# Latent attention: the weights' scaling by the reciprocal of their sums on GpSimd instead of VectorE

## The reference

```python
def mla_attention(q, k, v):
    # q, k: (B, S, 8, 96); v: (B, S, 8, 64)
    for blk in range(S // 128):
        qs, qe = blk * 128, (blk + 1) * 128
        logits = jnp.einsum('bqhd,bkhd->bhqk', q[:, qs:qe], k[:, :qe]) * scale
        logits = jnp.where(k_chunk <= q_chunk, logits, -jnp.inf)
        probs = jax.nn.softmax(logits, axis=-1)
        outs.append(jnp.einsum('bhqk,bkhd->bqhd', probs, v[:, :qe]))
```

## Time and profile before

| | us |
|---|---|
| median of three runs | 2461.8 |
| the profiled execution, first to last instruction (its span) | 2460.0 |
| TensorE busy in the span | 2419.9 (98%) |
| VectorE busy | 1705.1 (69%) |
| ScalarE busy | 1050.4 (43%) |
| GpSimd busy | 139.0 (6%) |
| the attention of the units, from its first scaling to its last values product | about 340 to 487 |

### The profile page before, as it was taken

One profiled execution on the slowest core, in us unless ns is written; L12 is line 12 of the kernel. 1 busy time (PEld: TensorE's weight loads), 2 busy tenths in 40 slices (PEclk: granted clock), 3 DMA queues, 4 the chain that ended last, 5 costly groups with the idle time before them and its releaser, 6 DMA issues.

```text
span 2460.0 us, 29760 instructions
## 1 busy us (share of the span) xinstructions
PE 2419.9 (98%) x11494; PEld 1921.0 (78%) x11494; DVE 1705.1 (69%) x2072; ACT 1050.4 (43%) x1495; POOL 139.0 (6%) x227
## 2 busy tenths in 40 slices
PE   8999999999999999999999999999999999999997
PEld 6887755588888888888788777788878888888885
DVE  5237888846877778698873665455588877786888
ACT  5225676624433333333542333343356333334336
POOL 1001100000000010000001000000001000100001
PEclk9999999999999999999999999999999999999999
DMA  5110000132433381600134122233444533715103
GB/s 220 52 43 22 2 1 1 52 137 107 150 119 121 103 307 53 222 1 18 52 100 151 43 78 70 72 133 134 148 150 175 171 103 103 263 45 194 47 1 137
DMA packets 76245, 252.22 MB, mean 103 GB/s; under 512 B 6320, under 2 KB 6368, under 8 KB 76080
## 3 DMA queue, kind: packets, MB, share of 16 engines
q1 hardware_dynamic: 43792, 131.08, 16.7%
q0 software_dynamic: 32320, 119.32, 13.0%
HBM read 186.78 MB, written 62.91 MB: 102 GB/s over the span
## 4 chain that ended last, share of the span: by engine, by line
PE 75%; DVE 10%; issue 4%; ACT 2%; DVEq 0%; ACTq 0%
PE ps L2717 23%; PE ps L3126 20%; PE ps L3164 18%; PE ps L3294 6%; DVE opQ_lo L2132 1%; DVE opQ_lo L2129 1%; DVE spot L2174 1%; DVE ql_raw L2169 1%; DVE Pb L1999 1%; PE ps L3221 1%; PE ps L3240 1%; PE ps L2965 1%; PE ps L3230 1%; PE ps L2839 0%; PE ps L2902 0%
## 5 line engine op out<-in xcount | busy, mean ns | idle before, releaser
L3164 PE MATMUL ps<-opQ_hi 128*128 128x512 f32 x896 | 350.3, 391 | 2.8 <-DVE opQ_lo L2132 2.8
L3164 PE MATMUL ps<-opQ_hi,opQ_lo 128*128 128x512 f32 x896 | 348.7, 389 | 0.0
L3164 PE MATMUL ps<-opQ_lo,opQ_hi 128*128 128x512 f32 x896 | 348.7, 389 | 0.0
L2717 PE MATMUL ps<-opP_hi,w_hi 128*128 128x512 f32 x638 | 199.2, 393 | 2.4 <-DVE w_lo L1620 0.7
L3164 PEld LDWEIGHTS ps<-opQ_hi 128*128 128x128 f32 x896 | 168.2, 188 | 42.1 <-DVE opQ_lo L2132 7.1
L2717 PE MATMUL ps<-opP_lo,w_hi 128*128 128x512 f32 x638 | 196.6, 389 | 0.0
L2717 PE MATMUL ps<-opP_hi,w_lo 128*128 128x512 f32 x638 | 196.4, 389 | 0.0
L3164 PEld LDWEIGHTS ps<-opQ_hi,opQ_lo 128*128 128x128 f32 x896 | 168.2, 188 | 35.1
L3164 PEld LDWEIGHTS ps<-opQ_lo,opQ_hi 128*128 128x128 f32 x896 | 168.2, 188 | 34.7 <-issue 0.2
L1276 ACT ACTIVATE opQ_hi<-spot 128x1024 fp32r<-128x1024 f32 x80 | 84.9, 1062 | 235.9 <-PE ps L3164 196.8
L884 ACT ACTIVATE w_hi<-w_stage 128x1024 fp32r<-128x1024 f32 x104 | 109.4, 1051 | 174.4 <-PE ps L2717 145.4
(11 more groups left out here) (441 smaller groups left out, 4763.0 us busy)
## 6 DMA issues: line engine op xcount, KB each, us to landing
w_stage<-in_w_stream SPq DMA_DIRECT2D x104, 512.0 KB, 3.7
h_spill<-T POOLq DMA_DIRECT2D x56, 512.0 KB, 4.5
pair_raw<-in_w_stream SPq DMA_DIRECT2D x26, 1024.0 KB, 5.8
spot<-in_w_stream SPq DMA_DIRECT2D x24, 1024.0 KB, 7.0
spot<-h_spill POOLq DMA_DIRECT2D x24, 1024.0 KB, 9.5
qh_raw<-in_w_stream SPq DMA_DIRECT2D x8, 1024.0 KB, 11.6
ql_raw<-h_spill POOLq DMA_DIRECT2D x8, 1024.0 KB, 7.5
g_spill<-T POOLq DMA_DIRECT2D x16, 512.0 KB, 2.9
```

The source lines that it names most:

```text
L2717: mm = pe.matmul(ps[:, psum + half, :], weight, operand[:, k, half * HALF:(half + 1) * HALF], start=(begin and x == 0 and weight is wh and ...
L3164: mm = pe.matmul(ps[:, down_bank(sc, f) + m, :], weight, operand, start=(g == 0 and kt == 0 and weight is wh and operand is hi), stop=(g = ...
```

## The change

The scaling leaves `normalise`, which keeps the reciprocal and its waits. GpSimd gets a loop over the 64 units, behind its additions: it waits for the reciprocal of the unit and scales the weights in place. The semaphores keep their meaning; `mha["pn"]` is now raised by GpSimd.

```diff
@@ GpSimd @@
                 ins.then_inc(g["pexp"], 1)
+
+            for u, (pr, qt, par) in enumerate(QBLOCKS):
+                width = (qt + 1) * P
+                pool.wait_ge(mha["rs"], u + 1)
+                pool.tensor_scalar(Pb[:, u % 4, 0:width], Pb[:, u % 4, 0:width], rsum[:, u % 4:u % 4 + 1], None, ALU.mult)\
+                    .then_inc(mha["pn"], 1)
@@ VectorE @@
             def normalise(u):
 
-                pr, qt, par = QBLOCKS[u]
-                width = (qt + 1) * P
                 v.wait_ge(mha["exp"], u + 1)
                 if u >= 4:
                     v.wait_ge(mha["pn"], u - 3)
                 v.reciprocal(rsum[:, u % 4:u % 4 + 1], esum[:, u % 4:u % 4 + 1]).then_inc(mha["rs"], 1)
-                v.wait_ge(mha["rs"], u + 1)
-                v.tensor_scalar(Pb[:, u % 4, 0:width], Pb[:, u % 4, 0:width], rsum[:, u % 4:u % 4 + 1], None, ALU.mult)\
-                 .then_inc(mha["pn"], 1)
```

## The result

| | before | after |
|---|---|---|
| median of the runs | 2461.8 us | 2489.8 us |
| the profiled execution's span | 2460.0 us | 2488.2 us |

The ratio is 1.0114, with a 95% interval of 1.0102 to 1.0126: slower by 28 us. The forecast was 2464 with a range of 2459 to 2476, so it was wrong, and by more than the slow rival (2477) allowed.

What follows compares the result with a forecast made beforehand. TensorE was taken as nearly full in attention, VectorE next. Four groups' shifts, −1.0 + 0.9 − 0.4 + 1.7, plus 1.2 of latency gave +2.4 us: 2460.0 to 2462.4, and 1.8 for the median, 2464.2; range 2459 to 2476.

Steps and rivals of the forecast that it cites:

- slow rival: GpSimd's scaling runs at the two-input rate, 2.03 ns an element: about +15 us, 2477; chance 0.30 with a half-slow case.
- Added: the GpSimd instruction: Price of one scaling on GpSimd, estimated near the memset's: 0.15 us + 0.86 ns an element, 1.03 us at 1024.
- upper bound: Highest price kept for a GpSimd scaling, from two-input rows at some 2.03 ns an element: 2.08 us at 1024.
- the prediction's own line between +2.4 and +15: Loss against GpSimd's time per element, from the forecast's +2.4 us to +15 at 2.03 ns; 1.45 ns gives some +8.7.
- No change: The outcome that the time stays within about 0.2%, 4.9 us, of the kernel before; chance 0.61.
- Added: a lock: In attention, 13 two-input VectorE extras starting just ahead of GpSimd's scaling hold it back 1.22 to 1.28 us each.
- Added: a hand-over: GpSimd starts 0.08 us after the VectorE instruction it awaits, against 0.04 within VectorE; uncovered latency costs 1.2 us in all.
- Removed from VectorE: 64 scalings, 33 us, leave VectorE in the attention stage; at most TensorE's 6.1 us of waiting could return.
- The cover: TensorE's other work hides the scaling in steps with a values product and the next; three places a group lose 0.3 us.
- The point of decision: The forecast is wrong if TensorE's wait for the scaling, 6.1 us before, falls under 2 us or rises over 12.

Runs made afterwards that it cites:

- e1: The changed kernel with GpSimd scaling only the first quarter of each unit's weights, the rest left unscaled: 2463.1 us beside 2461.6 for the kernel before.
- e3: The changed kernel with GpSimd's scaling written as a product of two tensors, the reciprocal broadcast along the row: 2472.1 us.
- e13: The changed kernel with one line moved, so VectorE takes the reciprocal of unit u+1 ahead of the row maximum of u+2: 2473.9 us.
- e8: The kernel before with seven chosen units scaled on GpSimd as a two-input product, the rest on VectorE: 2462.3 us beside 2460.0.
- e10: The kernel before with only the 16 units u % 4 = 2 scaled on GpSimd, each scaling also waiting for the one before it: 2474.8 us.
- e12: The kernel before with units u % 4 = 2 scaled on GpSimd, counted on its own semaphore, without waiting for the previous scaling: 2475.0 us.
- e9: The kernel before with only the 16 units u % 4 = 0 scaled on GpSimd, each scaling also waiting for the one before it: 2469.6 us.
- e11: The kernel before with units u % 4 = 0 scaled on GpSimd, counted on its own semaphore, without waiting for the previous scaling: 2467.4 us.
- e2: The changed kernel with GpSimd scaling only the first half of each unit's weights, the rest left unscaled: 2468.5 us.
- e15: The kernel before, scaling on VectorE, with reciprocal and scaling of unit u+1 moved ahead of the maximum of u+2: 2468.7 us.
- e14: The changed kernel with GpSimd scaling by a product of two tensors and the reciprocal moved ahead of the next maximum: 2463.8 us beside 2460.7.

## Why the prediction was wrong

**The step that failed** is "Added: the GpSimd instruction": "I take 0.15 us + 0.86 ns an element, an estimate: 1.03 us at 1024". It measured 0.28 us + 2.5 ns, 2.84 at 1024, above the upper bound of 2.08 too, and with it TensorE waited 30.5 us for scalings in place of 6.1. The memset was no near row: it writes only, with no arithmetic. e1 shows that the forecast held for a scaling of about the duration assumed. The rule that was weighed there, that of GPSIMD Engine Reference of the Trainium skill (Elementwise — side-by-side cycle accounting) with an estimated 0.88 us for 1024, is contradicted by the same rows, 2.84 us. Beside the slow rival the prediction set GPSIMD Engine Reference of the Trainium skill (When to use GPSIMD), which sends elementwise work to VectorE; the direction agrees with the trace. But that section calls work with one input roughly line-rate, and here it took 3.8 times VectorE's 0.753 us at 1024.

**The slow rival** had the right sign and a chance of 0.30. On the prediction's own line between +2.4 and +15, 1.66 ns an element gives an estimated 11 us, and e3 measured 10.3. Its rate was too low for the kernel after, but that is not all: on the same line 2.5 ns gives an estimated 20 us, and 28 were measured. The other 8 are the cover, below, and the lower clock. "No change" had 0.61 of the chances because both ends of the bound came from operations of another kind.

**Added: a lock.** It held where it was applied. The scalings behind two-input extras are longer by some 0.9 us (3.16 for 2.20, 3.42 for 2.52), the extras keep 1.27 and 1.20 us, and the one-input long reciprocals lock nothing, which the prediction assumed and SBUF — State Buffer of the Trainium skill (Who interferes with whom) says; the 0.93 us at 411.07 agree. Its net share of the time is small, 2.6 us by the medians, and not told from nothing. "Each time the later one stood until the earlier had finished" is too wide: e13's extra behind a one-input scaling did not stand.

**Added: a hand-over.** 0.10 us against the predicted 0.08.

**Removed from VectorE.** Busy time as predicted, 89.43. That it would return only what stood behind the scaling, 6.1 us at most, agrees with e8: 2.6 us of wait came back, and GpSimd's own delays took 4.0.

**The cover** ("in steps with V, and the step after, V covers it. That leaves three places in each group") failed as well, though at the assumed duration it didn't matter (e1). TensorE waited in 32 places, where it had waited in 15 before and 12 were to grow, and e10 and e12 show the "covered" units to cost more than the bare ones of e9 and e11. The cover was counted from the values product's length, without asking when in it the reciprocal comes.

**The point of decision.** "TensorE's wait ... over 12" was a good mark: of the kernels with scalings on GpSimd, those whose medians are over 0.2% longer are those from e2's 12.5 us up. e15 shows its limit, since there the delay stands before the scores.

What stays open: e14's median is 3.0 us longer with only 0.3 us more wait for scalings. Its profiled execution took 2462.2 us, among the shortest of runs that go up to 2468.2, and its span of 2460.5 is 0.5 over that of the kernel before; what the longer ones do, no trace shows. Open, too, is the exact share of the lock, since taking the extras out also takes out work, and how the 8 us beyond the prediction's line divide between the cover and the clock.

## What to carry to other kernels

A free engine is worth nothing to a chain that it makes slower: before moving an instruction off a busy engine, find the ring that it stands in and compare the ring's length, new duration included, with the work of the engine that bounds. A price for an operation that the trace doesn't show has to allow for a slow form: bounds from operations of another kind (a write, a product of two tensors) are no bounds. And if an instruction moves to another queue, ask again what should stand ahead of its input in the old queue: here the maximum ahead of the reciprocal was right with the scaling on VectorE (e15), and with it on GpSimd it cost 10 to 15 us (e13).

## What the runs showed of the hardware

- GpSimd's scaling of f32 rows by a factor takes 0.28 us + 2.5 ns an element (603 ns at 128, 2.84 us at 1024), 3.8 times VectorE's 0.753 at 1024; a constant factor saves 0.07 us in all. The product with the factor broadcast as a second tensor takes 0.19 us + 1.66 ns (400 ns at 128, 1.89 us at 1024).
- VectorE's one-input instructions mostly run at full speed beside GpSimd: the reciprocal 0.93 us, the scaling of 1024 in 0.75 us. Some scalings did not (1.14 in place of 0.62 us at 397.28 in e12); why isn't known.
- A two-input VectorE instruction that starts just ahead of GpSimd's scaling lengthens the scaling by about 0.9 us (3.16 for 2.20 at 768). One that starts in the middle of a one-input scaling takes its usual 1.28 us (e13); in the middle of a two-input product it took 1.60 for 1.22 (e14).
- TensorE's granted clock was 0.50 from 506.5 to 509.5 in the kernel after, after 2.87 us of waiting, and its busy time grew by 4.3 us for the same matmuls.
- A one-line change of queue order moved the time by 15 us in one direction and by 8 in the other, depending on the engine that scales.
